# A fused attention and pooling layer: values computed for four tiles across heads instead of three per head

## The chip, the cores and the metric

One core of a Trainium2 chip runs the whole layer in one launch. The metric is the device time of one execution in microseconds (us), as a median of repeated runs. TensorE's clock is granted at one of two levels, 1.2 or 2.4 GHz; the profiled execution shows 0.998 of the full one over its span.

## The reference, cut to what matters

One decoder layer on 256 tokens of width 2048, all in float32. One input projection gives, for 8 heads and 3 dilated groups, queries, keys and values of width 128, and further two gates and the input of a pooling branch:

```python
h = jnp.einsum('bsd,de->bse', x, w_in)
q, k, v, z_attn, u_pool, z_pool, g_pre = jnp.split(h, idx, axis=-1)
for g, (window, dilation) in enumerate(DILATED_GROUPS):      # 3 groups, 8 heads each
    o_g, lse_g = dilated_window_attention(q[:, :, g], k[:, :, g], v[:, :, g], window, dilation)
...
y_attn = o * jax.nn.silu(z_attn)
y_pool = causal_pool_mixer(u_pool, w_pool, pool_scale) * jax.nn.silu(z_pool)
g_attn, g_pool = jnp.split(jax.nn.sigmoid(g_pre + b_gate), 2, axis=-1)
merged = g_attn * (y_attn @ w_proj_attn) + g_pool * (y_pool @ w_proj_pool)
x = layer_norm(DEEPNORM_ALPHA * x + merged @ w_out, ln_gamma, ln_beta)
```

## The kernel before

All weights come as a stream of chunks of 1 MB (128 partitions x 2048 numbers) in a ring of three slots. SyncE loads chunk n into `w_raw` once the split of chunk n-3 is done. A product in float32 is made of parts: ScalarE rounds a chunk to `w_hi` (`split_hi`, two halves), VectorE forms the rest `w_lo = w_raw - w_hi` (`split_lo`, two halves), both two chunks ahead (`AHEAD`), and TensorE multiplies high and low parts and adds them up in PSUM. x lies split as `xt`.

A plain chunk (`chunk`) gives one tile of 128 output columns: 16 pairs of matmuls, one of 512 columns and one of 256, halved by a wait for each half of `w_lo`. Two banks of `proj_ps` take turns. ScalarE then copies one half of the sum out (`correction`, tile `corr`), and VectorE adds the other to it.

Phase A walks over the 8 heads, 12 chunks each (`head`): six for queries and keys of the three groups, three for the values (`values`: here x is the stationary operand, 96 matmuls of 384 columns, one for each of 16 k tiles, 2 token tiles and 3 parts), then `z_attn`, `u_pool` and `z_pool`. Between them TensorE works out the scores (`scores`, after the chunk with number 6, the first of the values), turns the probabilities (`turn_probs`, after the chunk with number 8, the last of the values) and, at the head's end, multiplies them with the values (`mix`). Head 0 is written out, heads 1 to 6 are a loop (`Fori`) on TensorE, ScalarE and VectorE, and head 7 is written out. Behind head 7 stand `pool_map` and the last `mix`. Phase B (gates and the two projections) and phase C (the output projection `w_out`, matmuls of 512 columns) follow.

VectorE does in each head, in the order of the program: the splits; the masked maximum of the scores (`masked_max`, tile `nmax`); after ScalarE's exponential (`exp_probs`) the division by the sum (`normalise`, tile `rden`); the low parts of values and turned probabilities (`v_lo`, `pt`); the gates (`sigmoid`: between `gate_f` and `gate` lies a tanh on ScalarE); and the pooling of the head's tile (`pool`, from `pool_a` to `p_lo`).

At the start the weights of chunks 0 to 2 come together with x in 8 pieces of two k tiles each (`PIECES`). `first_chunks` takes the first `SIDE_BY_SIDE` pieces for all three chunks in turn, and then what is left of chunk 0, of chunk 1 and of chunk 2. One piece for one chunk is called a step below: four matmuls, two of 512 columns and two of 256.

Of the kernel before, what the change touches and what calls it, by code (L numbers as in the profile page):

```python
# [27 lines left out]
P = 128  # L28
SEQ = 256
# [30 lines left out]
SIDE_BY_SIDE = 5  # L60
# [4 lines left out]
A_STEPS, A_CHUNKS = HEADS, 12  # L65
B_STEPS, B_CHUNKS = 4, 12

A_BANKED = A_CHUNKS - GROUPS
POOL_MAP = A_STEPS * A_CHUNKS
# [13 lines left out]
V_FIRST, Z_ATTN, U_POOL, Z_POOL = 6, 9, 10, 11  # L83
SCORES_AFTER, SOFTMAX_SUM, PT_AFTER, PT_SPLIT = 6, 7, 8, 9

assert V_FIRST % RING == 0 and GROUPS == RING
# [11 lines left out]
def banked(n, j):  # L98

    if n == 0:  # L100
        return j - min(max(j - V_FIRST, 0), GROUPS)
    return A_STEPS * A_BANKED + n - B_FIRST + j


def banked_per(n):

    return A_BANKED if n == 0 else B_CHUNKS


def layer_kernel(nc, first_d, x_d, stream_d, bias_d, scale_d, gamma_d, rows_d, row_kind_d, ident_d, mask_d,  # L110
                 coef_d, inv_d, beta_d, out_d):
    with ExitStack() as ctx:
# [12 lines left out]
        def place(at, items):  # L125
            made = []
            for name, shape, dt in items:
# [33 lines left out]
                    ("v_hi", [TT, GROUPS * P], F32R),  # L161
                    ("v_lo", [TT, GROUPS * P], F32R), ("mask", [TT, KEYS], F32),
# [35 lines left out]
        v_ps = (attn_ps[:, 1536:1536 + GROUPS * P], value_ps[:, 0:GROUPS * P])  # L198
# [146 lines left out]
        def _(pe):  # L345
# [3 lines left out]
            ring_hi = w_hi[:, :, :].rearrange("p r c -> p (r c)")  # L349
            ring_lo = w_lo[:, :, :].rearrange("p r c -> p (r c)")  # L350

# [101 lines left out]
            def values(j, i):  # L453

                n = V_FIRST + j

                pe.wait_ge(lo_split, 2 * n + 2 + i * (2 * A_CHUNKS))
                if j == 0:  # L460

                    pe.wait_ge(v_split, FROM + i * TT)
                before, upto = j * KT // GROUPS, (j + 1) * KT // GROUPS
                for k in range(before, upto):
                    cols = slice(k * GROUPS * P, (k + 1) * GROUPS * P)
                    for t in range(TT):
                        tokens = slice(t * P, (t + 1) * P)
                        done = product(v_ps[t][:, :], xt[:, k, 0, tokens], xt[:, k, 1, tokens],
                                       ring_hi[:, cols], ring_lo[:, cols], k == 0, k == KT - 1)
                    if j > 0 and k == before:  # L470

                        done.then_inc(chunk_done, 1)
                if j == GROUPS - 1:
                    done.then_inc(chunk_done, 1)

            def mix(i):

                pe.wait_ge(pt_split, FROM + i * PT_BANKS + PT_BANKS)
                pe.wait_ge(v_split, FROM + i * TT + TT)
# [5 lines left out]
                for g, kt in tiles:  # L485
                    v = slice(g * P, (g + 1) * P)
# [32 lines left out]
            def head(i, first):  # L519
                for j in range(A_CHUNKS):  # L520
# [3 lines left out]
                    elif V_FIRST <= j < V_FIRST + GROUPS:  # L524
                        values(j - V_FIRST, i)
                    elif first and j in APART:
                        chunk(0, j, i, A_CHUNKS, lambda k: (apart(ABREAST), xt[:, k, :, :], k == 0, k == KT - 1),
                              FIRST_TOGETHER)
                    else:
                        chunk(0, j, i, A_CHUNKS, from_x(j % 2), FIRST_TOGETHER if first and j < V_FIRST else A_TOGETHER)  # L530
                    if not (first and j < ABREAST):
                        next_bank(0, j, i)
# [93 lines left out]
        def _(act):  # L626
# [14 lines left out]
            def correction(n, j, i, per, pair=False, own_bank=False):  # L641
# [6 lines left out]
                else:  # L648
                    b = (n + j) % 2
                    source = (apart(j) if own_bank else proj_ps[:, b, :])[:, SEQ:2 * SEQ]  # L650
# [20 lines left out]
            def v_hi_parts(i):  # L671

                act.wait_ge(chunk_done, FROM + V_FIRST + GROUPS + i * A_CHUNKS)
                for t in range(TT):
                    activation(v_hi[:, t, :], v_ps[t][:, :], ACT.Copy).then_inc(v_hi_done, 1)

            def head(i, first):
                for j in range(A_CHUNKS):
                    if j == SOFTMAX_SUM:
                        exp_probs(i)  # L680
                    if j == PT_SPLIT:
                        for b in range(PT_BANKS):

                            act.wait_ge(pt_ready, i * PT_BANKS + b + 1)
                            activation(pt[:, b, 0, :], attn_ps[:, b * 512:(b + 1) * 512],
                                       ACT.Copy).then_inc(pt_hi_done, 1)
                    if not first or j > 0:
                        split_hi(0, j + AHEAD, i, A_CHUNKS)
                    if j == V_FIRST + GROUPS - 1:
                        v_hi_parts(i)  # L690
                    if j == Z_ATTN:

                        act.wait_ge(proj_free, FROM + banked(0, j) + i * A_BANKED)
                    if not V_FIRST <= j < V_FIRST + GROUPS:
                        correction(0, j, i, A_CHUNKS, own_bank=first and j in APART)
# [537 lines left out]
```

## Time and profile before

| | |
|---|---|
| median of 3 runs | 942.97 us (942.56 to 942.98) |
| profiled execution, own time | 943.06 us |
| its span, first to last instruction | 941.3 us |
| TensorE busy | 933.7 us, 99% of the span |
| VectorE busy | 635.5 us, 68% |
| ScalarE busy | 421.0 us, 45% |
| DMA | 178.30 MB, mean 189 GB/s |
| granted clock | 0.998 |

The busy time of TensorE counts overlapping matmuls once. The distance from the start of one matmul to that of the next is what a matmul costs; its own duration is longer, since the next starts while it drains.

### The profile page before, as it was taken

Reading aid. Unit: us, or ns where it says so; the run is one execution under the profiler, and the core shown is the slowest. Engines: PE = TensorE matmul, PEld = TensorE weight load, DVE = VectorE, ACT = ScalarE, POOL = GpSimd, SP = SyncE. Lnnn points to the kernel's source line nnn. Section 1 sums busy time; section 2 is a strip of 40 time slices with the busy share of each in tenths; the row PEclk is TensorE's granted clock in tenths of the full one; section 3 lists DMA queues with packets and bytes.
Section 4 is the critical chain, followed back from the end, with each engine's and each line's share of the span. In section 5 each row is a group of like instructions: output and inputs, shape, how many; then the busy total and the mean of one; then the engine's idle time right before and its main releaser. Section 6 shows DMA issues by size and latency. Waiting matters only on the chain.

```text
span 941.3 us, 14859 instructions
## 1 busy us (share of the span) xinstructions
PE 933.7 (99%) x5382; PEld 836.6 (89%) x5382; DVE 635.5 (68%) x1007; ACT 421.0 (45%) x589; POOL 0.2 (0%) x4
## 2 busy tenths in 40 slices
PE   9999999999999999999999999999999999999997
PEld 7998998998998998998998999888888888888886
DVE  7767567567567567567567567666666666666866
ACT  7354354354354354354354354545445444444340
POOL 0000000000000000000000000000000000000000
PEclk9999999999999999999999999999999999999999
DMA  9745545545545544544544545655555555557432
GB/s 374 262 154 182 198 158 182 194 160 181 193 161 181 189 164 178 190 167 178 186 171 179 186 173 224 224 182 209 190 178 185 183 211 178 185 199 287 178 134 90
DMA packets 26397, 178.30 MB, mean 189 GB/s; under 512 B 3327, under 2 KB 3583, under 8 KB 5759
## 3 DMA queue, kind: packets, MB, share of 16 engines
q1 hardware_dynamic: 25920, 173.72, 50.8%
q10 hardware_dynamic: 452, 4.24, 1.1%
q8 instruction: 17, 0.28, 0.1%
q14 instruction: 8, 0.07, 0.0%
HBM read 175.85 MB, written 2.10 MB: 189 GB/s over the span
## 4 chain that ended last, share of the span: by engine, by line
PE 97%; DMA 1%; DVE 1%; SPq 0%; ACT 0%; DVEq 0%; issue 0%
PE proj_ps L362 39%; PE proj_ps L366 20%; PE attn_ps L362 7%; PE attn_ps L354 4%; PE attn_ps L356 4%; PE attn_ps L355 4%; PE attn_ps L366 3%; PE value_ps L356 3%; PE value_ps L354 3%; PE value_ps L355 3%; DMA first_raw<-in_first 1%; PE mixed_ps L356 1%; PE mixed_ps L354 1%; PE mixed_ps L355 1%; PE mixed_ps L492 1%; PE attn_ps L429 1%
## 5 line engine op out<-in xcount | busy, mean ns | idle before, releaser
L362 PE MATMUL proj_ps<-xt,w_hi 128*128 128x512 f32 x1600 | 555.8, 392 | 0.0
L366 PE MATMUL proj_ps<-xt,w_lo 128*128 128x256 f32 x1600 | 444.3, 279 | 0.0
L787 DVE TENSOR_TENSOR w_lo<-w_raw,w_hi 128x1024 fp32r<-128x1024 f32 x314 | 369.2, 1219 | 71.5 <-ACT w_hi L631 69.9
L362 PEld LDWEIGHTS proj_ps<-xt,w_hi 128*128 128x128 f32 x1600 | 298.3, 187 | 65.0
L631 ACT ACTIVATE w_hi<-w_raw 128x1024 fp32r<-128x1024 f32 x314 | 314.2, 1051 | 42.2 <-PE mixed_ps L356 25.2
L366 PEld LDWEIGHTS proj_ps<-xt,w_lo 128*128 128x128 f32 x1600 | 302.0, 189 | 1.4
L651 ACT ACTIVATE corr<-proj_ps 128x256 f32<-128x256 f32 x102 | 39.1, 383 | 279.9 <-PE proj_ps L366 278.3
L801 DVE TENSOR_TENSOR qk_f<-proj_ps,corr 128x256 f32<-128x256 f32 x46 | 19.5, 423 | 76.0 <-ACT corr L651 76.0
L362 PE MATMUL attn_ps<-yp,w_hi 128*128 128x512 f32 x128 | 45.1, 391 | 0.0
L362 PE MATMUL attn_ps<-ya,w_hi 128*128 128x512 f32 x128 | 45.1, 391 | 0.0
L356 PE MATMUL value_ps<-w_hi,xt 128*128 128x384 f32 x128 | 42.9, 335 | 0.0
L354 PE MATMUL value_ps<-w_hi,xt 128*128 128x384 f32 x128 | 42.9, 335 | 0.0
L354 PE MATMUL attn_ps<-w_hi,xt 128*128 128x384 f32 x128 | 42.8, 335 | 0.0
L356 PE MATMUL attn_ps<-w_hi,xt 128*128 128x384 f32 x128 | 42.8, 335 | 0.0
L355 PE MATMUL value_ps<-w_lo,xt 128*128 128x384 f32 x128 | 42.8, 334 | 0.0
L355 PE MATMUL attn_ps<-w_lo,xt 128*128 128x384 f32 x128 | 42.8, 334 | 0.0
L801 DVE TENSOR_TENSOR gate_f<-proj_ps,corr 128x256 f32<-128x256 f32 x48 | 20.3, 423 | 27.9 <-ACT corr L651 27.5
L668 ACT ACTIVATE s_sb<-s_sb,nmax 128x512 f32<-128x512 f32 x16 | 11.4, 717 | 57.8 <-DVE nmax L849 57.8
L366 PE MATMUL attn_ps<-ya,w_lo 128*128 128x256 f32 x128 | 35.8, 280 | 0.0
L366 PE MATMUL attn_ps<-yp,w_lo 128*128 128x256 f32 x128 | 35.8, 280 | 0.0
L362 PEld LDWEIGHTS attn_ps<-ya,w_hi 128*128 128x128 f32 x128 | 23.9, 187 | 5.2
L362 PEld LDWEIGHTS attn_ps<-yp,w_hi 128*128 128x128 f32 x128 | 23.9, 187 | 5.2
(178 smaller groups left out, 955.0 us busy)
## 6 DMA issues: line engine op xcount, KB each, us to landing
w_raw<-in_weights SPq DMA_DIRECT2D x158, 1024.0 KB, 4.8
first_raw<-in_first SPq DMA_DIRECT2D x8, 640.0 KB, 8.2
res<-in_x_rows ACTq DMA_DIRECT2D x1, 2048.0 KB
out_rows<-res SPq DMA_DIRECT2D x8, 256.0 KB, 2.5
gamma<-in_gamma_row ACTq DMA_DIRECT2D x1, 1024.0 KB
beta<-in_beta_row ACTq DMA_DIRECT2D x1, 1024.0 KB
mask<-in_mask SPq DMA_DIRECT2D x1, 512.0 KB, 18.0
ident<-in_identity SPq DMA_DIRECT2D x1, 64.0 KB, 17.8
```

What stands on the lines that cost most here:

```text
L354: mm(out, a_hi, b_hi, start=first, stop=False)
L355: mm(out, a_hi, b_lo, start=False, stop=False)
L356: return mm(out, a_lo, b_hi, start=False, stop=last)
L362: mm(bank, w_hi[:, slot, k * P:(k + 1) * P], tile.rearrange("p a s -> p (a s)"), start=first, stop=False)
L366: done = mm(bank[:, SEQ:2 * SEQ], w_lo[:, slot, k * P:(k + 1) * P], tile[:, 0, :], start=False, stop=last)
L429: mm(out[:, :, cols], q_hi[:, g, q], keys[:, g, :, q], start=True, stop=False)
L492: mm(out[:, :, queries], v_hi[:, kt, v], pt[:, bank, :, cols], start=(g, kt) == tiles[0], stop=False)
L631: activation(w_hi[:, slot, cols], w_raw[:, slot, cols], ACT.Copy).then_inc(hi_split, 1)
L651: activation(corr[:, b, :], source, ACT.Copy).then_inc(act_evac, 1)
L668: activation(s_sb[:, t, :], s_sb[:, t, :], ACT.Exp, bias=nmax[:, t:t + 1], scale=SCALE, accum_out=den[:, t:t + 1]).then_inc(exp_done, 1)
L787: tt(w_lo[:, slot, cols], w_raw[:, slot, cols], w_hi[:, slot, cols].bitcast(F32), ALU.subtract).then_inc(lo_split, 1)
L801: tt(dst, source, corr[:, (n + j) % 2, :], ALU.add).then_inc(proj_free, 1)
```

## The change

The 24 tiles of values (3 groups x 8 heads) are no longer computed three per head but four at a time (`V_GROUP`), by 6 of the 8 heads. Such a head has four value chunks, each of 24 matmuls of 512 columns, and 13 chunks in all. Heads 3 and 7 compute none and have 9 chunks. All 96 chunks of phase A remain. The tiles lie in a buffer of six (`V_TILES`), where a group of four may wrap around, so that heads 1 and 5 write it in two runs per token tile.

In a head with values the scores still follow the first value chunk. In heads 3 and 7 the chunk after the keys is that of `u_pool`, and the scores stand between its two halves (`between`); the order is u, z_pool, z_attn. The turns of the probabilities stand behind the last value chunk, or behind the z_pool chunk in heads 3 and 7, one chunk after the scores' own. The mix now reads the values' tile of its head by number. `pool_map` waits for head 7's split probabilities and values too. At the start, six pieces stand abreast and not five. All eight heads are written out; the loop of phase A is gone.

```diff
-SIDE_BY_SIDE = 5
+SIDE_BY_SIDE = 6
...
+QK, V_GROUP, V_CHUNKS, V_TILES = 2 * GROUPS, 4, 4, 6
+A_BANKED = QK + 3
+def groups_by(h):
+    return -(-GROUPS * (h + 1) // V_GROUP)
+def has_values(h):
+    return groups_by(h) > groups_by(h - 1)
+def z_attn_at(h):
+    return QK + V_CHUNKS if has_values(h) else QK + 2
+def u_pool_at(h):
+    return z_attn_at(h) + 1 if has_values(h) else QK
+def z_pool_at(h):
+    return u_pool_at(h) + 1
+def turns_at(h):
+    return z_attn_at(h) - 1
...
-            def chunk(n, j, i, per, moving, together=A_TOGETHER):
+            def chunk(n, j, i, per, moving, together=A_TOGETHER, between=None):
...
+                    if half == 0 and between is not None:
+                        between()
...
-                before, upto = j * KT // GROUPS, (j + 1) * KT // GROUPS
-                for k in range(before, upto):
-                    cols = slice(k * GROUPS * P, (k + 1) * GROUPS * P)
+                for kk in range(BLOCK_KT):
+                    k, cols = c * BLOCK_KT + kk, slice(kk * BLOCK, (kk + 1) * BLOCK)
+                    if kk % 2 == 0:
+                        pe.wait_ge(lo_split, 2 * n + kk // 2 + 1)
                     for t in range(TT):
                         tokens = slice(t * P, (t + 1) * P)
                         done = product(v_ps[t][:, :], xt[:, k, 0, tokens], xt[:, k, 1, tokens],
-                                       ring_hi[:, cols], ring_lo[:, cols], k == 0, k == KT - 1)
+                                       w_hi[:, n % RING, cols], w_lo[:, n % RING, cols], k == 0, k == KT - 1)
...
             def pool_map():
...
+                pe.wait_ge(pt_split, FROM + A_STEPS * PT_BANKS)
+                pe.wait_ge(v_split, FROM + VALUE_PARTS[-1])
...
-                    if j == SCORES_AFTER:
+                    if j == SCORES_AFTER and has_values(i):
                         scores(i)
-                    if j == PT_AFTER:
+                    if j == turns_at(i):
                         turn_probs(i)
-            head(0, True)
-            mix(0)
-            with pe.Fori(1, A_STEPS - 1) as i:
-                head(i, False)
+            for i in range(A_STEPS - 1):
+                head(i, i == 0)
                 mix(i)
```

TensorE at the end of head 7's scores. `keys` and `q_hi`, `q_lo` make scores; `xt` with `w_hi`, `w_lo` in rows of 384 columns are values. Before:

```order
L429 MATMUL attn_ps<-keys,q_hi 128x2x128
L430 MATMUL attn_ps<-keys,q_lo 128x128
L354 MATMUL attn_ps<-keys,q_hi 128x256
L355 MATMUL attn_ps<-keys,q_hi 128x256
L356 MATMUL attn_ps<-keys,q_lo 128x256
L354 MATMUL attn_ps<-keys,q_hi 128x256
L355 MATMUL attn_ps<-keys,q_hi 128x256
L356 MATMUL attn_ps<-keys,q_lo 128x256
L354 MATMUL attn_ps<-w_hi,xt 128x384
L355 MATMUL attn_ps<-w_lo,xt 128x384
L356 MATMUL attn_ps<-w_hi,xt 128x384
```

After the change, where rows of 512 and 256 columns into `proj_ps` are the u_pool chunk:

```order
L480 MATMUL attn_ps<-keys,q_hi 128x2x128
L481 MATMUL attn_ps<-keys,q_lo 128x128
L403 MATMUL attn_ps<-keys,q_hi 128x256
L404 MATMUL attn_ps<-keys,q_hi 128x256
L405 MATMUL attn_ps<-keys,q_lo 128x256
L403 MATMUL attn_ps<-keys,q_hi 128x256
L404 MATMUL attn_ps<-keys,q_hi 128x256
L405 MATMUL attn_ps<-keys,q_lo 128x256
L411 MATMUL proj_ps<-xt,w_hi 128x512
L415 MATMUL proj_ps<-xt,w_lo 128x256
```

What follows the scores in this head is the second half of one plain chunk, no longer two more value chunks.

VectorE in head 7 from the scores' maximum on. `rden` and the `s_sb` row behind it are `normalise`, `v_lo` and `pt` the low parts that `mix` waits for. Before:

```order
L849 TENSOR_SCALAR nmax<-smax 128x2
L854 RECIPROCAL rden<-den 128x2
L856 TENSOR_SCALAR s_sb<-s_sb,rden 128x512 x2
L787 TENSOR_TENSOR w_lo<-w_raw,w_hi 128x1024 x4
L926 TENSOR_TENSOR v_lo<-attn_ps,v_hi 128x384
L926 TENSOR_TENSOR v_lo<-value_ps,v_hi 128x384
L900 TENSOR_TENSOR pt<-attn_ps,pt 128x512 x2
L787 TENSOR_TENSOR w_lo<-w_raw,w_hi 128x1024 x2
L801 TENSOR_TENSOR gate_f<-proj_ps,corr 128x256
L824 TENSOR_SCALAR gate<-th_gate 128x256
L921 TENSOR_TENSOR silu_za<-gate_f,gate 128x256
L787 TENSOR_TENSOR w_lo<-w_raw,w_hi 128x1024 x2
```

After the change, from the same place on:

```order
L896 TENSOR_SCALAR nmax<-smax 128x2
L988 TENSOR_TENSOR u_pad<-proj_ps,corr 128x2x128
L901 RECIPROCAL rden<-den 128x2
L903 TENSOR_SCALAR s_sb<-s_sb,rden 128x512 x2
L910 SCALAR_TENSOR_TENSOR pool_a<-u_pad,coef 128x256
L910 SCALAR_TENSOR_TENSOR pool_b<-pool_a,coef 128x256
L910 SCALAR_TENSOR_TENSOR pool_a<-pool_b,coef 128x256
```

and, four rows further on, the end of `pool` and what stands ahead of `pt`:

```order
L921 CAST p_hi<-sum_f 128x256
L922 TENSOR_TENSOR p_lo<-sum_f,p_hi 128x256
L834 TENSOR_TENSOR w_lo<-w_raw,w_hi 128x1024 x2
L848 TENSOR_TENSOR gate_f<-proj_ps,corr 128x256
L871 TENSOR_SCALAR gate<-th_gate 128x256
L993 SCALAR_TENSOR_TENSOR szp<-gate_f,pool_scale,gate 128x256
L941 TENSOR_TENSOR pt<-attn_ps,pt 128x512 x2
L834 TENSOR_TENSOR w_lo<-w_raw,w_hi 128x1024 x2
```

The evacuation of u and the whole of `pool`, a split and the z_pool gate moved in between the division and the low parts of the probabilities.

## Rows read from the trace of the kernel before

**Rows 1.** Page, part 1: engine, busy us (share of the span), instructions.

```profile
PE 933.7 (99%) x5382; PEld 836.6 (89%) x5382; DVE 635.5 (68%) x1007; ACT 421.0 (45%) x589; POOL 0.2 (0%) x4
```

**Rows 2.** Timeline of TensorE, head 0: start us, us, what.

```profile
47.76 0.33 PE L354 MATMUL attn_ps<-w_hi,xt 128*128 128x384 f32 x1
...
58.16 0.60 PE L444 MATMUL attn_ps<-ident,s_sb 128*128 128x128 f32 x4
...
64.58 0.39 PE L362 MATMUL proj_ps<-xt,w_hi 128*128 128x512 f32 x1
...
70.13 0.39 PE L362 MATMUL proj_ps<-xt,w_hi 128*128 128x512 f32 x1
```

**Rows 3.** Timeline of TensorE, output projection; 18 matmuls apart.

```profile
849.85 0.39 PE L354 MATMUL value_ps<-w_hi,merged 128*128 128x512 f32 x1
...
853.93 0.39 PE L354 MATMUL value_ps<-w_hi,merged 128*128 128x512 f32 x1
```

**Rows 4.** Timeline of TensorE, the first chunks.

```profile
16.85 0.62 PE L399 MATMUL proj_ps<-xt,w_hi 128*128 128x512 f32 x2
...
18.61 0.51 PE L403 MATMUL proj_ps<-xt,w_lo 128*128 128x256 f32 x2 [0.18 <-DVE w_lo L814]
18.95 0.63 PE L399 MATMUL proj_ps<-xt,w_hi 128*128 128x512 f32 x2
...
23.14 0.63 PE L362 MATMUL attn_ps<-xt,w_hi 128*128 128x512 f32 x2
```

**Rows 5.** Timeline of VectorE, the first chunks.

```profile
17.59 0.96 DVE L814 TENSOR_TENSOR w_lo<-first_raw,w_hi 128x768 fp32r<-128x768 f32 x1
...
20.77 2.35 DVE L787 TENSOR_TENSOR w_lo<-w_raw,w_hi 128x1024 fp32r<-128x1024 f32 x2
```

**Rows 6.** Timeline of ScalarE, head 0.

```profile
49.51 0.73 ACT L668 ACTIVATE s_sb<-s_sb,nmax 128x512 f32<-128x512 f32 x1 [7.18 <-DVE nmax L849]
...
70.33 0.38 ACT L651 ACTIVATE corr<-proj_ps 128x256 f32<-128x256 f32 x1 [2.23 <-PE proj_ps L366]
70.61 2.00 ACT L631 ACTIVATE w_hi<-w_raw 128x1024 fp32r<-128x1024 f32 x2
```

**Rows 7.** Timeline of VectorE, head 0.

```profile
46.89 0.69 DVE L832 TENSOR_TENSOR s_sb<-attn_ps,mask 128x512 f32<-128x512 f32 x1 [2.93 <-PE attn_ps L356]
...
52.07 4.62 DVE L787 TENSOR_TENSOR w_lo<-w_raw,w_hi 128x1024 fp32r<-128x1024 f32 x4
...
59.82 1.28 DVE L900 TENSOR_TENSOR pt<-attn_ps,pt 128x512 fp32r<-128x512 f32 x2
...
71.20 0.48 DVE L863 SCALAR_TENSOR_TENSOR pool_a<-u_pad,coef 128x256 f32<-128x256 f32 x1
...
74.75 2.35 DVE L787 TENSOR_TENSOR w_lo<-w_raw,w_hi 128x1024 fp32r<-128x1024 f32 x2
77.02 0.42 DVE L801 TENSOR_TENSOR gate_f<-proj_ps,corr 128x256 f32<-128x256 f32 x1
...
78.72 0.41 DVE L944 TENSOR_TENSOR mixed_f<-mixed_ps,mixed_corr 128x256 f32<-128x256 f32 x1
```

**Rows 8.** Timeline of VectorE, head 3, inside the loop.

```profile
283.50 0.48 DVE L863 SCALAR_TENSOR_TENSOR pool_a<-u_pad,coef 128x256 f32<-128x256 f32 x1 [0.15 <-DVE u_pad L932]
...
287.71 2.35 DVE L787 TENSOR_TENSOR w_lo<-w_raw,w_hi 128x1024 fp32r<-128x1024 f32 x2
```

**Rows 9.** Chain of waits: the probabilities' turns of heads 5, 6, 7.

```profile
411.95 0.44 PE attn_ps L444 x4
...
482.68 0.44 PE attn_ps L444 x4
...
553.41 0.44 PE attn_ps L444 x4
```

**Rows 10.** Page, part 3: an instruction queue over the whole span.

```profile
q8 instruction: 17, 0.28, 0.1%
```

**Rows 11.** The same queue, 160 to 520 us: packets, MB, share.

```profile
q8 instruction: 1, 0.02, 0.0%
```

More of the change, by code:

```diff
@@ L63, with a_chunks, value_runs @@
 PIECE_COLS = SEQ + ABREAST * P
-A_STEPS, A_CHUNKS = HEADS, 12
+A_STEPS = HEADS
 B_STEPS, B_CHUNKS = 4, 12
-A_BANKED = A_CHUNKS - GROUPS
-POOL_MAP = A_STEPS * A_CHUNKS
+QK, V_GROUP, V_CHUNKS, V_TILES = 2 * GROUPS, 4, 4, 6
[4 more added lines that the diff above has]
+    return groups_by(h) > groups_by(h - 1)
+def a_chunks(h):
+    return A_BANKED + V_CHUNKS * has_values(h)
+def z_attn_at(h):
[6 more added lines that the diff above has]
+    return z_attn_at(h) - 1
+START = [sum(a_chunks(h) for h in range(before)) for before in range(A_STEPS + 1)]
+POOL_MAP = START[A_STEPS]
+BANKED = [A_BANKED * h + (j if j < QK else max(j - (a_chunks(h) - A_BANKED), QK))
+          for h in range(A_STEPS) for j in range(a_chunks(h))]
+def value_runs(group):
+    first = group * V_GROUP % V_TILES
+    fits = min(V_GROUP, V_TILES - first)
+    runs = [(0, first, fits)] + ([(fits, 0, V_GROUP - fits)] if fits < V_GROUP else [])
+    return [tuple(P * tile for tile in run) for run in runs]
 B_FIRST = POOL_MAP + 1
@@ L81 @@
 FROM = 1
-V_FIRST, Z_ATTN, U_POOL, Z_POOL = 6, 9, 10, 11
-SCORES_AFTER, SOFTMAX_SUM, PT_AFTER, PT_SPLIT = 6, 7, 8, 9
-assert V_FIRST % RING == 0 and GROUPS == RING
+SCORES_AFTER, SOFTMAX_SUM = QK, QK + 1
+VALUE_PARTS = [TT * sum(len(value_runs(g)) for g in range(before)) for before in range(groups_by(A_STEPS - 1) + 1)]
 KEYS = SEQ + (GROUPS - 1) * P
@@ L519, in head @@
             def head(i, first):
-                for j in range(A_CHUNKS):
+                for j in range(a_chunks(i)):
+                    n = START[i] + j
                     if first and j < ABREAST:
@@ L677, in head, with pt_hi_parts @@
+            def pt_hi_parts(i):
+                for b in range(PT_BANKS):
+                    act.wait_ge(pt_ready, i * PT_BANKS + b + 1)
+                    activation(pt[:, b, 0, :], attn_ps[:, b * 512:(b + 1) * 512],
+                               ACT.Copy).then_inc(pt_hi_done, 1)
             def head(i, first):
-                for j in range(A_CHUNKS):
+                for j in range(a_chunks(i)):
+                    n = START[i] + j
                     if j == SOFTMAX_SUM:
                         exp_probs(i)
[L681 to L686, printed above, removed]
+                    if j == turns_at(i) + 1:
+                        pt_hi_parts(i)
@@ L687, in head @@
                     if not first or j > 0:
-                        split_hi(0, j + AHEAD, i, A_CHUNKS)
-                    if j == V_FIRST + GROUPS - 1:
+                        split_hi(n, AHEAD, 0, 0)
+                    if j == z_attn_at(i) - 1 and has_values(i):
                         v_hi_parts(i)
[L691 to L695, printed above, removed]
@@ L696, in head @@
-                    if j in (Z_ATTN, Z_POOL):
-                        act.wait_ge(proj_free, FROM + banked(0, j) + 1 + i * A_BANKED)
-                        z = int(j == Z_POOL)
+                    if j < QK or j >= QK + V_CHUNKS * has_values(i):
+                        correction(n, 0, 0, 0, own_bank=first and j in APART)
+                    if j in (z_attn_at(i), z_pool_at(i)):
+                        act.wait_ge(proj_free, FROM + banked(n, 0) + 1)
+                        z = int(j == z_pool_at(i))
@@ L705, in mix_correction @@
                 activation(mixed_corr[:, :], mixed_ps[:, SEQ:2 * SEQ], ACT.Copy).then_inc(mixed_corr_done, 1)
-            head(0, True)
-            mix_correction(0)
-            with act.Fori(1, A_STEPS - 1) as i:
-                head(i, False)
+            for i in range(A_STEPS - 1):
+                head(i, i == 0)
                 mix_correction(i)
@@ L947, in gated_mix @@
                 split(mixed_f[:, :], ya, i, y_split)
-            head(0, True)
-            gated_mix(0)
-            assert chain.count - start_a == per_a, chain.count - start_a
-            chain.count, chain.per = start_a, per_a
-            with dve.Fori(1, A_STEPS - 1) as i:
-                chain.i = i
-                head(i, False)
+            for i in range(A_STEPS - 1):
+                head(i, i == 0)
                 gated_mix(i)
-            assert chain.count - start_a == per_a, chain.count - start_a
-            chain.count, chain.i = start_a, A_STEPS - 1
             head(A_STEPS - 1, False)
@@ L1172, in _stream @@
                 stream[n + j] = cols[tile].reshape(P, CHUNK)
-        values = cols[2 * qkv + h:3 * qkv:HEADS].transpose(1, 2, 0, 3).reshape(P, GROUPS, CHUNK)
-        stream[n + V_FIRST:n + V_FIRST + GROUPS] = values.transpose(1, 0, 2)
-        n += A_CHUNKS
+        if has_values(h):
+            group = range(V_GROUP * (groups_by(h) - 1), V_GROUP * groups_by(h))
+            values = cols[[2 * qkv + tile % GROUPS * HEADS + tile // GROUPS for tile in group]]
+            values = values.transpose(1, 2, 0, 3).reshape(P, V_CHUNKS, CHUNK)
+            stream[n + QK:n + QK + V_CHUNKS] = values.transpose(1, 0, 2)
+        n += a_chunks(h)
     stream[n] = w_pool.reshape(4, 2, P, POOL_GROUP).transpose(2, 0, 1, 3).reshape(P, CHUNK)
```

133 lines of the change are left out of this document (70 added, 63 removed).

## The prediction

> **What bounds the kernel now.** I read the page's busy times first: TensorE is busy 933.7 of 941.3 us [rows 1]. Then its timeline. Matmul follows matmul at a fixed distance through all of phase A, B and C, and the only waits inside are a few tenths of a microsecond at the start and at the very end. So the time is the sum of TensorE's distances from start to start, and a change can do three things: change that sum, remove a wait, or bring one in. VectorE and ScalarE have gaps and matter only where TensorE comes to wait for them.
>
> What one matmul costs: the last 60 value matmuls of head 0 run from 47.76 to 58.16 us [rows 2], 0.1733 us each for 384 columns. In the output projection 18 matmuls of 512 columns take 4.08 us [rows 3], 0.2267 each. The difference is 0.0533 us for 128 columns, which is 2.4 GHz; what is left, 0.0133 us, is a fixed cost of each matmul. A plain chunk takes 5.55 us (64.58 to 70.13), and the turns with the chunk behind them 6.42 (58.16 to 64.58), so the turns alone 0.87 [rows 2].
>
> **The change, part by part.**
>
> *Values.* Before, 8 heads x 96 matmuls x 0.1733 = 133.1 us. After, 6 x 96 x 0.2267 = 130.6 us. The columns are the same, 192 matmuls are gone, and each takes its 0.0133 us with it: 2.56 us less. The form (512 moving columns, a stationary tile of 128x128) is that of the output projection, whose chunks of 24 matmuls also last 5.44 us and are fed by the same splits with no wait, so I take its price. Scores, turns, mix and plain chunks keep number and form.
>
> The Trainium skill, TensorE: Matmul & The Clock Gate, section Back-to-back issue gap, gives an isolated warm matmul as N/2.4 + 2.5 ns. By that the 192 matmuls would be worth 0.48 us and not 2.56. The trace does not agree: its fixed part is 13.3 ns at 384 and at 512 columns alike [rows 2, 3].
>
> *The start, six pieces abreast.* A step normally takes 0.698 us (six steps from 18.95 to 23.14). The two steps from 16.85 take 2.10, so 0.70 is lost: the low part of the last piece is done on VectorE at 17.59 + 0.96 = 18.55, and TensorE goes on at 18.61 [rows 4, 5]. The release costs 0.06, and the two matmuls behind it take 0.34 where 0.24 is normal (the 0.698 of a step less two of 0.2267, rounded), so 0.10 more, since their weights aren't loaded ahead. After the change chunk 0 meets its last piece two steps later in the line, in step 20 rather than 18. It would start at 16.85 + 3 x 0.698 = 18.94, after the 18.55. So the 0.70 is gone, chunk 0 ends at 19.64 (before: 18.95) and chunk 3 could start at 22.43 (before: 23.14).
>
> But chunk 3 needs its first low half, which VectorE starts 1.82 us after the end of chunk 0 (20.77 against 18.95) and ends about 1.2 later (two take 2.35) [rows 4, 5]. After the change that is 19.64 + 1.82 + 1.22 = 22.68, with release and weight load 22.84: a new wait of 0.41. Left of the start: 0.70 - 0.41 = **0.29 us gained**. The chunks behind have room: the next low half is due 5.5 us later and takes 3.4 more of VectorE's time.
>
> *Scores inside u's chunk (heads 3 and 7).* They need the last key split, 1.82 us after the end of its chunk by the same rows (correction, sum, cast, rest). Half a chunk, 2.77 us, covers it. Cost nothing; without the cover it would be the difference.
>
> *The mix in heads 3 and 7.* This is the critical place. Before, the low parts of the turned probabilities were done three chunks ahead of the mix. Now everything between the u chunk and the mix is two chunks and the turns: 5.55 + 0.87 + 5.55 = **11.97 us** on TensorE. Against it stands a chain over ScalarE and VectorE, counted from the end of the u chunk, with the order of the rows of the change:
> - ScalarE starts u's correction 0.20 later (70.13 to 70.33) and the next instruction, now the exponential, 0.28 after that [rows 2, 6]. The maximum isn't late: from the start of the masking to the exponential 2.62 pass (46.89 to 49.51) [rows 6, 7], with 0.20 ahead of it 2.82 from the end of the scores, where u's second half and correction take 2.77 + 0.48.
> - exponential and division, to VectorE's next instruction: 2.56 (49.51 to 52.07) [rows 6, 7]
> - pool: 3.55 (71.20 to 74.75)
> - split of the next chunk: 2.27 (74.75 to 77.02)
> - z_pool's gate, with the tanh on ScalarE in between: 1.70 (77.02 to 78.72)
> - the two low parts of `pt`: 1.28 [rows 7]
> - release 0.06 and weights 0.10 [rows 4, 5]
>
> The sum is 12.00 us, a wait of 0.03 in each of the two heads, 0.06 in all. That is a tie. These prices are from head 0, which is written out, as all heads are after the change. Inside the loop the pool takes 4.21 us rather than 3.55 [rows 8], and with that the chain is 12.66 and the wait 0.69. I take the written-out price, since nothing in the changed code reads a loop register there. In head 7 the same wait stands ahead of `pool_map`, at the same distance; it needs nothing later. The mix's stall would not spread: the splits of the next two chunks are due 1.6 and 7 us after the mix begins.
>
> *Heads with values.* From scores to turns lie three value chunks (3 x 5.44 = 16.3 us) where 11.3 were (46.89 to 58.16) [rows 2, 7], and the value parts get 2 x 512 columns or, in heads 1 and 5, four pieces of 256. All are due at the mix, three chunks (16.6 us) on. Nothing.
>
> *The loop.* TensorE pays nothing for it now: from the turns of head 5 to those of head 6 it is 70.73 us, all in the loop, and from head 6 to head 7, 52 us of it written out, 70.73 again [rows 9]. Nothing gained and, if code arrives in time, nothing lost. The stream, the number of chunks and the ring slots are as before.
>
> **The sum.** -2.56 - 0.29 + 0.06 = -2.79 us against the profiled execution's own 943.06, so 940.27. The median of the runs shown, 942.97, is 0.09 below it, so I say **940.2 us**, 0.3% less.
>
> **Rivals.**
> 1. *The tie is lost.* Heads 3 and 7 wait at the loop's prices, 0.69 each: 1.32 more, **941.5 us**, within 0.2%. For it: the margin is a rounding error and any added wait counts double. Against: both written-out places show the 3.55. Chance 0.13.
> 2. *Code doesn't arrive in time; slower.* An instruction queue moved 17 packets in the whole span but one between 160 and 520 us, where the loop ran [rows 10, 11]. Written out, some 18 more must come, each amid weight traffic. If each stopped TensorE by x, the kernel gets slower by 0.2% once 18x exceeds 2.79 + 1.89, so from x = 0.26 us on, about **944.9 us**. Against: 52 us of head 7, where packets do come, cost TensorE nothing [rows 9]. Chance 0.04. The Trainium skill, Runtime: NRT & Kernel Launch, section Instruction fetch mechanics, holds that sequential code is fetched ahead and that only taken branches break this. The equal heads agree.
> 3. *The fixed cost stays.* Value matmuls of 512 columns take 3.6 ns more than those of the output projection, so that only 2.5 ns for each of the 192 is saved, 0.48 in place of 2.56: **942.3 us**. The page on TensorE named above would have it so; two column counts in the trace speak against it. Chance 0.04.
> 4. *The start gives another amount.* With no new wait 0.70 is gained (939.9 us, inside the forecast's own range); if chunk 3 waits 0.7 or more, or the 0.29 and part of the tie are both lost, 940.8 to 941.4. Chance of the latter 0.09.
>
> The forecast's own case, 939.8 to 940.7, has 0.70.
>
> **How the numbers follow.** A measurement of this kernel tells about 0.2%, 1.9 us, from no change; the border lies at 941.1. The forecast and half of rival 4 lie below it, and with part of rival 1 (one head waits, 940.9) that is 0.78 for faster. Within 0.2%: the rest of rivals 1 and 4, rival 3, 0.17. Slower: rival 2 and what I have overlooked, 0.05. The range takes in the best start (939.9, less 0.2 for the spread between runs) and both waits of rival 1: 939.7 to 941.6.
>
> **What the changed profile would show.** Value matmuls 0.2267 apart. TensorE without a wait at 17 to 19 us and with one of about 0.4 just before chunk 3, near 22.5. In heads 3 and 7 either none or a few hundredths ahead of the mix and `pool_map`, VectorE's `pt` named as the releaser if any; `pool` at 3.55 us in every head. Heads with values 75.85 us long and head 3 54.1 (the 70.73 of now less 96 x 0.1733, and plus 96 x 0.2267 or nothing). The prediction is wrong if TensorE shows waits in any other place, or if the distance of 512-column value matmuls isn't that of phase C.

## The result, and the profile after

The change made the kernel slower, by 0.35%. Its median is 946.43 us (945.56 to 946.69 in 7 runs) against 942.94 us before (942.56 to 943.06 in 7 runs). The ratio is 1.0035, with an interval of 1.0025 to 1.0045. The forecast of 940.2 us and its range both missed.

The page of the changed kernel answers to [rows 1] and [rows 10]: busy us by engine, and the instruction queue.

```profile
span 944.9 us, 13719 instructions
...
PE 938.1 (99%) x5190; PEld 813.7 (86%) x5190; DVE 634.5 (67%) x1007; ACT 419.9 (44%) x589; POOL 0.2 (0%) x4
...
q8 instruction: 32, 0.52, 0.2%
```

TensorE has the 192 matmuls fewer, and is busy 4.4 us longer. Its waits don't explain that. This is the whole answer on what it waited for (times are in total, count, longest):

```profile
PE mixed_ps L545 <- DVE zeros L853: 1.8, 1, 1.8
PE attn_ps L667 <- ACT shift_rows L805: 0.4, 1, 0.4
PE value_ps L662 <- DVE shift_parts L1165: 0.2, 1, 0.2
```

One is at the very start and two are at the very end, as before. So I went by distances. The chain of waits gives the turns of each head, which answer to [rows 9]:

```profile
64.00 0.43 PE attn_ps L495 x4
...
140.80 0.44 PE attn_ps L495 x4
...
217.60 0.44 PE attn_ps L495 x4
...
283.90 0.44 PE attn_ps L495 x4
...
348.80 0.44 PE attn_ps L495 x4
```

A head with values lasts 76.80 us (head 4, counted from mix to mix, 76.21), where I had forecast 75.85: 0.95 too much in each but that one. It isn't the values. In the value chunks TensorE takes 21.80 us per head (5.46 for the first chunk, 16.34 for the three others) where it took 16.675, and 8 x 16.675 - 6 x 21.80 = 2.6 us less, as forecast. It is the plain chunks, which the change doesn't touch. Here are two stretches of 32 us that hold plain chunks alone, in head 1 and in head 4 (busy us and count for each engine, then the granted clock, the DMA share and GB/s):

```profile
84.00:116.00 32.00, 32.00 (x183) 27.75 (x182) 21.47 (x33) 13.40 (x18) 0.00 (x0) 1.00 0.57 198
293.00:325.00 32.00, 32.00 (x186) 28.23 (x186) 21.55 (x33) 13.60 (x19) 0.00 (x0) 1.00 0.60 199
```

TensorE is never idle in either and the granted clock is 1.00 (2.4 GHz), yet it gets through 183 matmuls in one and 186 in the other. In the timeline of TensorE in the first of them, a pair (512 and 256 columns) is mostly 0.36 and sometimes 0.34 us behind the last one:

```profile
84.00 0.40 PE L411 MATMUL proj_ps<-xt,w_hi 128*128 128x512 f32 x1
84.24 0.28 PE L415 MATMUL proj_ps<-xt,w_lo 128*128 128x256 f32 x1
84.36 0.40 PE L411 MATMUL proj_ps<-xt,w_hi 128*128 128x512 f32 x1
84.59 0.28 PE L415 MATMUL proj_ps<-xt,w_lo 128*128 128x256 f32 x1
84.70 0.40 PE L411 MATMUL proj_ps<-xt,w_hi 128*128 128x512 f32 x1
84.94 0.28 PE L415 MATMUL proj_ps<-xt,w_lo 128*128 128x256 f32 x1
85.06 0.40 PE L411 MATMUL proj_ps<-xt,w_hi 128*128 128x512 f32 x1
```

Three pairs repeat at 1.06 us there, and at 1.04 before the change. A chunk of 16 pairs so takes 5.65 us in place of 5.55 [rows 2]. I call these **the 5.65 pace and the 5.55 pace**. Before the change every plain chunk of both phases keeps the 5.55 pace. After the change, the six chunks ahead of the values take 33.92 us instead of 33.29 in heads 1, 2, 5 and 6 (4 x 0.63); the 6.5 ahead of the scores take 36.74 in heads 3 and 7, where 36.06 is their time at the 5.55 pace, as in `e3_nudges` below (2 x 0.67), and what follows there 0.24 more each; the three chunks behind the turns of the six heads with values take 17.04 instead of 16.72 (6 x 0.32). Together 6.2 us. Head 4's six chunks and all of phase B keep the 5.55 pace.

Two more places differ. The start, which answers to [rows 4] and [rows 5], in the timelines of TensorE and then VectorE:

```profile
5.41 1.15 PE L450 MATMUL proj_ps<-xt,w_hi 128*128 128x512 f32 x2
...
7.94 0.62 PE L450 MATMUL attn_ps<-xt,w_hi 128*128 128x512 f32 x2
...
22.57 0.63 PE L450 MATMUL attn_ps<-xt,w_hi 128*128 128x512 f32 x2
...
23.57 0.73 PE L411 MATMUL attn_ps<-xt,w_hi 128*128 128x512 f32 x2
```

```profile
22.30 2.36 DVE L834 TENSOR_TENSOR w_lo<-w_raw,w_hi 128x1024 fp32r<-128x1024 f32 x2
```

The first two steps of TensorE before the change:

```profile
5.41 0.90 PE L399 MATMUL proj_ps<-xt,w_hi 128*128 128x512 f32 x2
...
7.08 0.63 PE L399 MATMUL attn_ps<-xt,w_hi 128*128 128x512 f32 x2
```

The wait at the last piece of chunk 0 is gone. With a step of 0.70 from 22.57 chunk 3 could start at 23.27. It starts at 23.57, and its first matmul is followed 0.11 late (0.34 after it where 0.23 is normal), so the wait costs the forecast 0.41. But the first two steps take 2.53 us (5.41 to 7.94) where before they took 1.67 (5.41 to 7.08): up to 7.7 us the 512-column matmuls here still follow at 0.43 us, which is 512 columns at 1.2 GHz, though the granted clock of the window 5 to 8 us reads 1.00. That is 0.86 more, and 0.86 - 0.70 + 0.41 is 0.57. The first value matmul comes at 40.41 us, where it came at 39.86.

And the end. This is what the queue of SyncE waited for at the end of the program, before and after the change:

```profile
SPq L112 <- DMA out_rows<-res: 2.5, 1, 2.5
```

```profile
SPq L164 <- DMA out_rows<-res: 1.8, 1, 1.8
```

Before the change 5.3 us passed from the start of TensorE's last matmul to the end of the span, where it now is 4.6 (940.26 to 944.9). TensorE itself is 4.3 us later; 0.7 of that came back in the last transfer.

So the ledger on TensorE is: values -2.6, start +0.6, plain chunks +6.2, which makes +4.2 of the 4.3 measured, and then -0.7 at the end. That gives +3.6 between the two profiled executions and +3.5 between the medians.

### The profile page after: what moved, and what is told of

Same layout as the page of the kernel before. It is cut to its first block, busy times and chain, and to the rows that moved or that the text cites. A ratio compares the mean times of both kernels' runs of the same rounds, so it can differ in the third digit from the quotient of the medians.

```text
span 944.9 us, 13719 instructions
## 1 busy us (share of the span) xinstructions
PE 938.1 (99%) x5190; PEld 813.7 (86%) x5190; DVE 634.5 (67%) x1007; ACT 419.9 (44%) x589; POOL 0.2 (0%) x4
## 4 chain that ended last, share of the span: by engine, by line
PE 99%; DVE 1%; issue 0%; DVEq 0%; ACT 0%
PE proj_ps L411 39%; PE proj_ps L415 20%; PE attn_ps L411 7%; PE attn_ps L403 4%; PE attn_ps L405 4%; PE attn_ps L404 4%; PE attn_ps L415 3%; PE value_ps L405 3%; PE value_ps L403 3%; PE value_ps L404 3%; PE mixed_ps L405 1%; PE mixed_ps L403 1%; PE mixed_ps L536 1%; PE mixed_ps L404 1%; PE proj_ps L450 1%; PE attn_ps L480 1%
## 5 line engine op out<-in xcount | busy, mean ns | idle before, releaser
L411 PE MATMUL proj_ps<-xt,w_hi 128*128 128x512 f32 x1600 | 562.1, 396 | 0.0
L403 PE MATMUL attn_ps<-w_hi,xt 128*128 128x512 f32 x96 | 37.4, 390 | 0.0
L405 PE MATMUL value_ps<-w_hi,xt 128*128 128x512 f32 x96 | 37.4, 390 | 0.0
L404 PE MATMUL attn_ps<-w_lo,xt 128*128 128x512 f32 x96 | 37.4, 390 | 0.0
L405 PE MATMUL attn_ps<-w_hi,xt 128*128 128x512 f32 x96 | 37.4, 389 | 0.0
L404 PE MATMUL value_ps<-w_lo,xt 128*128 128x512 f32 x96 | 37.3, 389 | 0.0
L403 PE MATMUL value_ps<-w_hi,xt 128*128 128x512 f32 x96 | 37.3, 389 | 0.0
```

Source lines behind the costliest of these rows:

```text
L403: mm(out, a_hi, b_hi, start=first, stop=False)
L404: mm(out, a_hi, b_lo, start=False, stop=False)
L405: return mm(out, a_lo, b_hi, start=False, stop=last)
L411: mm(bank, w_hi[:, slot, k * P:(k + 1) * P], tile.rearrange("p a s -> p (a s)"), start=first, stop=False)
```

## The experiments

**First: is it the loop, or the start?** If writing the loop out were what slows the chunks, the kernel before with its loop written out would show it. `e1_written_out` is the kernel before with this one edit, on three engines:

```diff
-            head(0, True)
-            mix(0)
-            with pe.Fori(1, A_STEPS - 1) as i:
-                head(i, False)
+            for i in range(A_STEPS - 1):
+                head(i, i == 0)
```

> The kernel before, with nothing but the loop of phase A written out on TensorE, ScalarE and VectorE. In the profile of the changed kernel the six plain chunks of a head take 33.92 us in heads 1, 2, 5, 6 (33.29 in head 4 and in every head of before), and a plain chunk pair of matmuls 353 ns where 347 were. Theory P (a pace that the values of 512 columns and the turns hand on to the plain chunks): 33.29 in every head here, time within 0.3 us of before, 943.0. Theory W (written-out code is fed more slowly): 33.9 in most heads, some 5 to 6 us more, 948.

Measured: 942.37 us (942.02 to 942.85, 10 runs) against 943.0 beside it, ratio 0.9994 (0.9984 to 1.0003). Each head has 33.29 and 16.72 us as before. A stretch of head 2 in it, by windows:

```profile
149.00:181.00 32.00, 32.00 (x186) 28.23 (x185) 21.21 (x32) 13.10 (x17) 0.00 (x0) 1.00 0.56 197
```

So fetching the code costs TensorE nothing, and theory W falls. The Trainium skill, Runtime: NRT & Kernel Launch, section Instruction fetch mechanics, says that straight code is fetched ahead; this run agrees, with no longer chunk anywhere. What the edit does change is the end: SyncE's queue waits 1.8 us for the last output as in the changed kernel, and 4.6 us pass from TensorE's last matmul. All eleven kernels of mine without the loop have 4.6 us there; the two with it, before and `e12_before_shift_b`, have 5.3 and 5.4. That is 0.7 us gained which I had not seen.

`e2_five` is the changed kernel with the start of before:

```diff
-SIDE_BY_SIDE = 6
+SIDE_BY_SIDE = 5
```

> The changed kernel with five pieces abreast as before. By the prediction's term for the start it is 0.29 us slower than the changed kernel; both theories on the pace expect the same heads of 76.8 us. In the profile of the changed kernel TensorE ran cold until 7.8 us (5.4 in before) and lost about 0.9 us by it. If six pieces brought that about, this one is warm from 5.4 us on and about 0.6 us faster than the changed kernel; if it is a matter of the moment, the time of the start varies from run to run.

Measured: 946.05 us (945.74 to 946.37, 6 runs), ratio 1.0033 (1.002 to 1.0045). All heads are as in the changed kernel, 33.92 us for six chunks included, so the start has no part in the pace. With five pieces abreast the kernel is 0.4 us faster than the changed one, where the prediction's term made it 0.29 slower. Its first two steps take 1.55 us (5.82 to 7.37). Yet it isn't six pieces abreast that bring the late full clock: `e12_before_shift_b`, below, has the start of before, and its first two steps take 2.50 us (5.41 to 7.91).

**Second: does what stands right ahead of the chunks set their pace?** These kernels put one more matmul behind the turns, whose result nothing uses, so that the chunks behind start a little later. The edit, with its widths in columns for heads 0 to 7 in `e3_nudges`:

```diff
+NUDGE_TURNS = (0, 16, 32, 0, 64, 96, 128, 0)
...
+            def nudge(i, width):
+                if width:
+                    pe.wait_ge(mixed_free, FROM + i)
+                    mm(mixed_ps[:, 0:width], xt[:, 0, 0, 0:P], xt[:, 0, 0, 0:width], start=True, stop=True)
...
+                        nudge(i, NUDGE_TURNS[i])
```

> The changed kernel with one extra matmul of 16, 32, 64, 96 and 128 columns behind the turns of heads 1, 2, 4, 5 and 6, into a free bank of mixed_ps; it computes nothing that is used. Each costs under 0.1 us by itself. Theory P: the extra matmul shifts the phase in which the plain chunks begin, so that in some of these heads the three plain chunks behind it take 16.7 us instead of 17.04, and the next head's six 33.3 instead of 33.92. Theory W: nothing but the added matmuls changes, 17.0 and 33.9 stay everywhere.

Measured: 943.00 us in one run, 3.4 less than the changed kernel, with five matmuls more. Windows of plain chunks in head 2 and in head 1:

```profile
160.00:192.00 32.00, 32.00 (x187) 28.23 (x185) 21.61 (x33) 13.88 (x19) 0.00 (x0) 1.00 0.55 197
84.00:116.00 32.00, 32.00 (x183) 27.75 (x182) 21.05 (x32) 12.94 (x17) 0.00 (x0) 1.00 0.54 194
```

Head 1's chunks, behind head 0 which had no extra matmul, keep the 5.65 pace. Head 2's, behind the first one with an extra matmul of 16 columns, keep the 5.55 pace. `e6_map` tries other widths, `e5_all_64` has 64 columns in all six heads with values, and `e8_before_nudged` is `e1_written_out` with widths 0, 8, 16, 32, 48, 64, 96, 0.

> The changed kernel with one extra matmul of 64 columns, which computes nothing that is used, behind the turns of all six heads with values. Theory P: as head 4 with it in the run before, the three plain chunks behind take 16.73 instead of 17.04, the next head's six 33.29 instead of 33.92, at 0.11 for the extra matmul: 5 heads x 0.83 (one of them, head 2, is followed by head 3 with seven fast chunks) and 0.2 more for the sixth, less 0.6 because head 4 then begins slow: about 3.5 to 4 us less than the changed kernel, 942.5. A rival, that the shift worked there only by the state which the heads before had left: some heads stay slow, 944 to 945.

> The changed kernel with the extra matmul of 48, 56, 80, 160, 256 and 192 columns behind the turns of heads 0, 1, 2, 4, 5, 6, and of 64 in heads 3 and 7; it computes nothing that is used. Known so far: 0, 16 and 32 columns leave the three chunks behind at 17.04 to 17.05, 64 and more give 16.70 to 16.73. If the phase is what counts and repeats with a period, some of 80 to 256 are slow again; if only a minimum of distance from the turns counts, everything from some width between 32 and 64 on is fast.

> The kernel before, its loop written out, values of 384 columns and all, with an extra matmul of 8, 16, 32, 48, 64 and 96 columns behind the turns of heads 1 to 6, which computes nothing that is used. Theory P in its wide form (the phase decides, whatever caused it): some of these heads fall into the slow pace, 17.0 for three chunks and 33.9 for the next six, in a kernel that has none of the change. If the slow pace needs 512-column values ahead, all stay at 16.72 and 33.29.

What the three chunks behind the turns and the next six took, in us, by the width of the extra matmul:

```
columns          0     8     16    32    48    56    64    80    96    128   160   192   256
changed, three   17.04 -     17.05 17.05 17.05 16.73 16.73 16.73 16.71 16.70 16.68 16.67 16.97
changed, six     33.92 -     33.29 33.29 33.29 33.29 33.29 33.29 33.29 33.29 33.29 33.29 33.29
before, three    16.72 17.04 17.04 17.04 17.04 -     17.05 -     17.04 -     -     -     -
before, six      33.29 33.92 33.92 33.92 33.92 -     33.29 -     33.29 -     -     -     -
```

(The six are those of the next head, taken from its 6.5 where that is head 3 or 7. Head 4's six have a case of their own, below. A - is a width not tried. Each width stands for one head of one run, only 0 and 64 for more. With 256 columns three chunks take 16.97 because their first pair is shorter; one by one they take 5.65, 5.66 and 5.66, which is the 5.65 pace.) With 8 columns the kernel before itself falls into the 5.65 pace. Windows of it, head 2 and then head 1:

```profile
149.00:181.00 32.00, 32.00 (x183) 27.72 (x182) 21.31 (x33) 13.26 (x17) 0.00 (x0) 1.00 0.56 196
77.00:109.00 32.00, 32.00 (x186) 28.22 (x186) 21.71 (x34) 13.99 (x19) 0.00 (x0) 1.00 0.56 198
```

So 512-column value matmuls aren't needed for the 5.65 pace, and written-out code alone doesn't bring it.

By how much does the extra matmul delay the chunks? In `e6_map` head 0 has one of 48 columns and keeps the 5.65 pace behind it; head 1 has one of 56 and changes to 5.55:

```profile
64.15 0.27 PE L569 MATMUL mixed_ps<-xt 128*128 128x48 f32 x1
64.26 0.48 PE L412 MATMUL proj_ps<-xt,w_hi 128*128 128x512 f32 x1
...
140.47 0.27 PE L569 MATMUL mixed_ps<-xt 128*128 128x56 f32 x1
140.58 0.48 PE L412 MATMUL proj_ps<-xt,w_hi 128*128 128x512 f32 x1
```

In both, and for all widths from 8 to 80, the chunk's first matmul follows the extra one by 0.11 us. The delay is the same to a hundredth of a microsecond and the pace isn't. So what decides is finer than that, or it isn't the delay.

`e8_before_nudged` took 947.97 us and `e6_map` 946.8, one run each. In `e5_all_64` seven runs gave a median of 946.56 (ratio 1.0041, 1.0026 to 1.0055), but they fell in two groups: 941.42 and 941.96, and five from 946.47 to 947.15. Its profile is of the run of 941.96, where all plain chunks but head 4's six (33.91 us) keep the 5.55 pace.

**Third: the same by order alone.** `e4_turns_later` adds no matmul; it moves the turns of the heads with values one plain chunk further, and `e7_later_five` is the same with five abreast:

```diff
-    return z_attn_at(h) - 1
+    return z_attn_at(h) - (not has_values(h))
```

> The changed kernel with the turns of the probabilities one plain chunk later in heads with values, so that a plain chunk follows the last value chunk directly. Theory P, if the turns set the slow pace: z_attn's chunk runs at 5.55 us and the chunks behind the turns as slow as now, or all at 5.55 if it takes both. If the 512-column values set it: 5.65 from z_attn's chunk on. Theory W: 5.65 for all, as now.

> The changed kernel with the turns one plain chunk later in heads with values, and five pieces abreast. With six abreast the same order took 941.74 once. By the prediction's term for the start five are 0.29 slower (942.0). By what the profiles of six kernels show, five abreast reach the first value chunk at 39.69 to 39.85 us and six at 39.94 to 40.41, since the wait for the last piece takes up a late start and the wait of 0.41 before chunk 3 comes on top: 0.1 to 0.6 faster, 941.4.

Measured: `e4_turns_later` 941.74 us in one run. The chunk right behind the values takes 5.65 us in every head and is at the 5.65 pace; the two behind the turns take 11.18 together (twice 5.55 and a slower first pair), and the next six 33.29, except in head 4, 33.92. Head 4's six are at the 5.65 pace in all four kernels in which TensorE, at the 5.55 pace in head 3, meets a small wait at that head's mix (`e3_nudges`, `e4_turns_later`, `e5_all_64`, `e7_later_five`: 0.25 or 0.26 us between two matmuls where 0.23 is normal), and at 5.55 in those that have none there. `e7_later_five` is alike in phase A. Its ten runs gave 946.56 at the median, ratio 1.0019 (1.0 to 1.0037), again in two groups: three from 940.64 to 941.55 and seven from 946.47 to 946.75. The profiled one is of the slower group. Its TensorE and then its VectorE at the tie in head 7:

```profile
569.38 0.40 PE L411 MATMUL proj_ps<-xt,w_hi 128*128 128x512 f32 x1
569.62 0.28 PE L415 MATMUL proj_ps<-xt,w_lo 128*128 128x256 f32 x1
569.86 0.36 PE L403 MATMUL attn_ps<-p_hi,w_hi 128*128 128x256 f32 x1
570.05 0.28 PE L404 MATMUL attn_ps<-p_lo,w_hi 128*128 128x256 f32 x1
```

```profile
568.32 1.28 DVE L941 TENSOR_TENSOR pt<-attn_ps,pt 128x512 fp32r<-128x512 f32 x2
```

The first matmul of `pool_map` comes 0.24 us after the last one of the chunk where 0.12 is normal, and the next 0.19 after that: 0.2 us is lost, to `pt`, which ends at 569.60. This is the wait of 0.03 that I had forecast. Behind it all of phase B keeps the 5.65 pace. A window of 240 us inside phase B, before the change and then in `e7_later_five`:

```profile
600.00:840.00 240.00, 240.00 (x1387) 211.65 (x1386) 157.05 (x218) 116.39 (x159) 0.00 (x0) 1.00 0.53 191
600.00:840.00 240.00, 240.00 (x1360) 208.12 (x1359) 153.58 (x213) 115.16 (x158) 0.00 (x0) 1.00 0.53 186
```

There are 1360 matmuls in it, where before the change, and in the changed kernel, there are 1387 and 1386. Phase B takes 271.4 us (577.31 to 848.66) in place of the 266.25 of before. The pace is steady: from 583 to 843 us each three pairs take 1.060 us, and 1.039 to 1.041 before the change, whatever VectorE, ScalarE and the DMA engines do meanwhile. That speaks against contention with them. The changed kernel has no wait at the tie, for its 5.65 pace brings TensorE there later.

A wait there doesn't settle the pace by itself. `e3_nudges`, `e4_turns_later` and `e5_all_64` lose the same 0.2 us at the tie, and phase B keeps the 5.55 pace in their profiled runs. `e6_map` loses 0.1 us there, and its phase B takes 271.4 us, 5.1 of the 946.8 us that it took.

**Fourth: phase B by itself.** `e12_before_shift_b` is the kernel before, loop and all, with one matmul of 48 columns between the last mix and phase B:

```diff
+            mm(value_ps[:, 0:48], xt[:, 0, 0, 0:P], xt[:, 0, 0, 0:48], start=True, stop=True)
```

> The kernel before, loops and all, with one extra matmul of 48 columns between the last mix and phase B, which computes nothing that is used. If the phase in which B starts decides its pace, B can fall to 11.30 us for two plain chunks, and the kernel takes up to 5 us more, 948, for 0.03 us of work. If the pace of B needs something of the change, 943.0.

Its timeline of TensorE there, and the same window of phase B as above:

```profile
578.22 0.18 PE L546 MATMUL value_ps<-xt 128*128 128x48 f32 x1
578.24 0.47 PE L362 MATMUL proj_ps<-xt,w_hi 128*128 128x512 f32 x1
```

```profile
600.00:840.00 240.00, 240.00 (x1360) 208.02 (x1359) 154.23 (x215) 113.94 (x156) 0.00 (x0) 1.00 0.53 187
```

Measured: 948.40 us in one run against 943.02 beside it. A matmul of some 20 ns goes with 5.4 us more, since each of the 48 chunks behind it takes 0.1 more. It is one run, but none of the 53 runs of the kernel before on record took more than 943.34 us.

**Fifth: take the tie away.** In heads 3 and 7 the parts of the turned probabilities are made ahead of `z_pool`'s gate rather than behind it, on ScalarE and on VectorE, so that TensorE doesn't come to wait for them:

```diff
-                    if j == turns_at(i) + 1:
+                    if j == turns_at(i) + 1 and has_values(i):
...
+                    if j == turns_at(i) and not has_values(i):
+                        pt_lo_parts(i)
```

`e9_pt_early_five` is `e7_later_five` with this, `e10_pt_early_six` is `e4_turns_later` with it, and `e11_after_pt_early` is the changed kernel with it.

> As the kernel with the turns one chunk later and five pieces abreast, whose runs fell on 940.6 to 941.6 and on 946.5 to 946.8, but in heads 3 and 7 the parts of the turned probabilities are worked out ahead of the z_pool gate on ScalarE and VectorE, some 1.7 us before the mix and pool_map ask for them. Theory L (the small wait of about 0.15 us ahead of pool_map, released by VectorE at a moment that isn't TensorE's own, throws the phase in which phase B starts, and so 11.09 or 11.30 us for two chunks in all of B, 5 us): the wait is gone and the runs lie within 0.5 us of each other, at either 940.5 or 946. Rival: the phase is drawn elsewhere, as by the start; then the runs stay split in two groups 5 us apart.

> The same with six pieces abreast. By the prediction's term 0.29 faster than with five; by the profiles' times at which the values begin 0.1 to 0.6 slower. By theory L again one group of runs.

> The changed kernel with nothing but the parts of the probabilities of heads 3 and 7 worked out earlier. Its heads are slow, so that TensorE comes to the mix 0.2 us later than the low parts are done and doesn't wait there today. Theory P: nothing changes before the end of head 3, and no more than the pace of one head or of B behind; 946 if B stays fast, 951 if it is slow.

TensorE and VectorE of `e9_pt_early_five` at the same place in head 7, and its phase B:

```profile
568.80 0.28 PE L415 MATMUL proj_ps<-xt,w_lo 128*128 128x256 f32 x1
568.92 0.28 PE L403 MATMUL attn_ps<-p_hi,w_hi 128*128 128x256 f32 x1
569.04 0.28 PE L404 MATMUL attn_ps<-p_lo,w_hi 128*128 128x256 f32 x1
```

```profile
565.78 1.28 DVE L943 TENSOR_TENSOR pt<-attn_ps,pt 128x512 fp32r<-128x512 f32 x2
```

```profile
600.00:840.00 240.00, 240.00 (x1387) 211.59 (x1386) 155.57 (x217) 117.79 (x161) 0.00 (x0) 1.00 0.54 191
```

`pt` is done two microseconds early, there is no gap ahead of `pool_map`, and phase B keeps the 5.55 pace. Measured: `e9_pt_early_five` **940.41 us** (940.35 to 940.78, 8 runs), ratio 0.9973 (0.9962 to 0.9983), and `e10_pt_early_six` 940.85 (940.58 to 941.56, 10 runs), ratio 0.9979 (0.9969 to 0.9988). Neither has a run in a second group, and both beat the kernel before, by 0.3 and 0.2%. They were timed on another chip than the two kernels with two groups. The 14 runs of the kernel before on the chip of the two groups lie within 942.76 to 943.34 us, so the chip alone doesn't make them; but whether `e9_pt_early_five` would stay in one group on it wasn't tried. `e11_after_pt_early` took 946.25 in one run, its heads as in the changed kernel: the tie is not what slows the changed kernel.

## Why the prediction was wrong

- **The step that failed** is the last sentence on the values: "Scores, turns, mix and plain chunks keep number and form". They do keep them, and I took that to mean that they keep their price. I had read one price of a plain chunk, 5.55 us [rows 2], and every chunk of before has it, so no row there showed that another exists. In the changed kernel 5.65 turns up in every head, and that costs 6.2 us. Nothing else reaches the size of the miss. That nothing inside the chunk sets its pace is shown: in the kernel before, extra matmuls of 8 to 48 columns bring the 5.65 pace, and in the changed kernel the later turns end it behind them without any matmul more or less. That it is the moment at which the chunks start which counts is argued, not shown. Nor is it shown which part of the change brings it. The loop (`e1_written_out`), the start (`e2_five`) and the tie (`e11_after_pt_early`) are out; what is left is the value chunks of 512 columns ahead of the turns, and no kernel has those alone.
- **Values**: -2.56 forecast, -2.6 measured. The output projection was the right row to price them by [rows 3], and rival 3 (the fixed cost stays) is out: 0.2267 us each.
- **The start**: its new wait of 0.41 was right, and the sum was not. I forecast the first value chunk 0.29 us earlier; with six abreast it came at 39.92 to 40.41 us in seven kernels, with five at 39.52 to 39.95 in seven. What was missing: the first wait, at a time that data sets, also swallowed a late start of TensorE's full clock, and without it such a lateness counts. `e12_before_shift_b`, with five abreast, takes 0.83 us more than before for its first two steps, has no wait at the last piece, and starts its first value matmul only 0.09 later (39.95). And `e9_pt_early_five` against `e10_pt_early_six`, which differ in nothing else, is 940.41 against 940.85: here six abreast costs 0.4 us. It is a term of the wrong sign by about 0.7, second to the plain chunks.
- **The tie**: `pool` takes 3.55 (565.91 to 569.46 after the change). In `e7_later_five`, with the plain chunks at 5.55, u's chunk ends at 557.76 and `pt` at 569.60: 11.84 us, as forecast. The last term was too small: TensorE goes on 0.26 behind `pt`, not 0.16, and its next matmul comes 0.07 late. So the wait is 0.2 us in place of 0.03; in the changed kernel itself the 5.65 pace hides it. Rival 1 was right to distrust this place, but priced it by its own length (1.3 us for both heads). In `e7_later_five` a wait of 0.2 us there goes with a phase B that is 5 us longer in the profiled run, and by their times in six more of ten.
- **The loop**: TensorE pays nothing, as said, though the instruction queue moved 32 packets and not 17. Rival 2, the slower case, had its size within reach (944.9 us) and its mechanism wrong. What I left out was a gain of 0.7 at the last output transfer.
- The changed profile's signs that I had named did their work. "Heads with values 75.85 us long" failed, with no wait and no value matmul to blame, and so pointed at the plain chunks.

That the two groups of runs need the small wait at the tie is borne out by taking it away, in two kernels with 18 runs, none in the slower group (the chip was another one, as said). That the wait does it by coming at a slightly different moment in each run is argued, not shown. What stays open is which property of the moment, if it is the moment, counts: the widths have no simple order (in the kernel before, 0 and 8 are on different sides; in the changed one 48 is at the 5.65 pace, 56 to 192 at 5.55 and 256 at 5.65 again), so the outcome of a given shift can't be worked out from these runs.

## What to carry to other kernels

Where an engine is busy all the time, measure the same unchanged block in every place where it stands, before and after: "not touched" is no price, and a block that repeats a hundred times turns 0.1 us into more than the change was worth. Count matmuls per window of equal length beside the granted clock, since no wait and no clock shows such a loss. And don't let the busiest engine arrive in a dead heat with another, however short the wait: give the other room, as the early `pt` did with 1.9 us.

## What the runs showed of the hardware

- The same 32 matmuls (512 and 256 columns in turn, each with weights of its own) run at two steady paces, 346.7 and 353.3 ns a pair, at a granted clock of 1.00 in both. A pace holds through a whole run of chunks: through 48 of them in phase B.
- One matmul of 48 columns ahead of them came with the slower one, at 5.4 us in one run (`e12_before_shift_b`).
- An extra matmul of 8 to 80 columns behind the turns put the next one 0.11 us later at each of these widths, whatever the columns.
- One and the same kernel gave times in two groups 5 us apart (`e5_all_64`, `e7_later_five`) where TensorE met a wait of 0.2 us ahead of a long run of chunks; without the wait there was one group (`e9_pt_early_five`, `e10_pt_early_six`).
- The last output transfers ended 0.7 us earlier in all kernels with the loop written out. With the loop the last outputs took 2.7 us to land and without it 2.1 (before and `e1_written_out`, medians of four). One microsecond of it, 938 to 939 before the change, moved 311 GB/s at a DMA share of 1.05; after the change 942.3 to 943.3 moved 375 at 1.00. Why the loop does that is open.
